# Both feed-forwards of a hybrid encoder layer by one level of Strassen's method

## The reference

```python
def swiglu(h, w_gate, w_up, w_down):
    return (jax.nn.silu(h @ w_gate) * (h @ w_up)) @ w_down

x = x + 0.5 * swiglu(rmsnorm(x, norm_ffn1), w1_gate, w1_up, w1_down)   # D_FF = 2816
x = x + token_mix(rmsnorm(x, norm_mix))      # SSD, GLA and forgetting attention, w_in and w_out
x = x + 0.5 * swiglu(rmsnorm(x, norm_ffn2), w2_gate, w2_up, w2_down)
```

## Time and profile before

| | |
|---|---|
| median of three runs | 2297.13 us |
| profiled execution: span | 2299.3 us |
| TensorE busy, matmuls | 2238.2 us (97%), 13579 |
| VectorE, ScalarE, GpSimd busy | 938.9, 537.3, 215.4 us |
| DMA: moved, mean rate | 112.34 MB, 49 GB/s |
| first feed-forward's last matmul ends | 823.9 us |
| second feed-forward's last matmul ends | 2295.6 us |

### The profile page before, as it was taken

The page is one execution under the profiler, slowest core; times in us unless marked ns, Lnnn a source line. Parts: engine busy times, 40 slices in busy tenths (PEclk is TensorE's granted clock), DMA queues, the critical chain, the costliest instruction groups (busy, mean ns, idle before and its releaser), DMA issues.

```text
span 2299.3 us, 32648 instructions
## 1 busy us (share of the span) xinstructions
PE 2238.2 (97%) x13579; PEld 2149.2 (93%) x13579; DVE 938.9 (41%) x1630; ACT 537.3 (23%) x887; POOL 215.4 (9%) x255
## 2 busy tenths in 40 slices
PE   7999999999999989999999999989999999999999
PEld 6999999999999979768889978989999999999999
DVE  5234324342243472455544294252333323333235
ACT  5211111111111252543232243231111111111110
POOL 2000000000000060231121073220000000000000
PEclk9999999999999999999999999999999999999999
DMA  4111111111111122101011103111111111111111
GB/s 152 55 38 39 36 56 55 39 37 37 56 47 46 38 79 92 58 1 37 20 39 38 42 2 124 37 37 37 55 37 56 37 37 56 37 56 37 37 56 79
DMA packets 19151, 112.34 MB, mean 49 GB/s; under 512 B 2184, under 2 KB 5736, under 8 KB 7616
## 3 DMA queue, kind: packets, MB, share of 16 engines
q1 hardware_dynamic: 16800, 97.04, 12.2%
q0 software_dynamic: 2208, 13.14, 1.5%
HBM read 98.40 MB, written 11.77 MB: 48 GB/s over the span
## 4 chain that ended last, share of the span: by engine, by line
PE 91%; DVE 5%; ACT 2%; issue 2%; POOL 1%; DMA 0%; DVEq 0%; POOLq 0%; ACTq 0%
PE ps L126 83%; DVE sb_nrm L228 2%; PE ps L650 2%; PE ps L689 2%; PE ps L662 1%; DVE sb_nl L214 1%; DVE sb_seg L1334 1%; PE ps L632 0%; ACT sb_whi L108 0%; PE ps L1150 0%; POOL sb_rms L154 0%; PE ps L949 0%; PE ps L927 0%; DVE sb_seg L1374 0%; PE ps L618 0%
## 5 line engine op out<-in xcount | busy, mean ns | idle before, releaser
L126 PE MATMUL ps<-sb_nh,sb_whi 128*128 128x362 f32 (+1 forms) x2808 | 929.7, 331 | 26.6 <-ACT sb_sg L346 8.4
L126 PE MATMUL ps<-sb_nl,sb_whi 128*128 128x362 f32 (+1 forms) x2808 | 924.8, 329 | 0.0
L126 PE MATMUL ps<-sb_nh,sb_wlo 128*128 128x362 f32 (+1 forms) x2808 | 924.8, 329 | 0.0
L126 PEld LDWEIGHTS ps<-sb_nh,sb_whi 128*128 128x128 f32 x2808 | 531.6, 189 | 36.4 <-issue 11.4
L126 PEld LDWEIGHTS ps<-sb_nl,sb_whi 128*128 128x128 f32 x2808 | 531.9, 189 | 0.5 <-issue 0.3
L126 PEld LDWEIGHTS ps<-sb_nh,sb_wlo 128*128 128x128 f32 x2808 | 531.3, 189 | 0.0
L380 DVE TENSOR_TENSOR sb_h<-sb_sg,ps 128x364 f32<-128x364 f32 x132 | 70.1, 533 | 759.4 <-PE ps L126 657.5
L393 DVE SCALAR_TENSOR_TENSOR sb_x<-ps,sb_x 128x364 f32<-128x364 f32 x528 | 276.4, 533 | 177.2 <-PE ps L126 177.2
L126 PE MATMUL ps<-sb_hh,sb_whi 128*128 128x362 f32 (+1 forms) x1056 | 345.4, 327 | 0.0
L126 PE MATMUL ps<-sb_hl,sb_whi 128*128 128x362 f32 (+1 forms) x1056 | 344.7, 326 | 0.0
L126 PE MATMUL ps<-sb_hh,sb_wlo 128*128 128x362 f32 (+1 forms) x1056 | 344.2, 326 | 0.0
(11 more groups left out here) (225 smaller groups left out, 1372.0 us busy)
## 6 DMA issues: line engine op xcount, KB each, us to landing
sb_wraw<-weights SPq DMA_DIRECT2D x83, 1024.0 KB, 4.9
x_kept<-sb_x POOLq DMA_DIRECT2D x1, 4352.0 KB, 14.3
sb_x<-x_kept POOLq DMA_DIRECT2D x4, 1088.0 KB, 10.1
out_y<-sb_x SPq DMA_DIRECT2D x8, 544.0 KB, 2.7
sb_x<-x SPq DMA_DIRECT2D x2, 1448.0 KB, 12.8
sb_x<-x SPq DMA_DIRECT2D x1, 1456.0 KB, 6.7
out_k<-sb_fk POOLq DMA_DIRECT2D x1, 1088.0 KB, 7.1
out_v<-sb_fv POOLq DMA_DIRECT2D x1, 1024.0 KB, 5.4
```

What stands on the lines that cost most here:

```text
L126: mm = K.nc.tensor.matmul(out, a, b, start=first and n == 0, stop=last and n == 2)
```

## The change

Each feed-forward's two matrix products are computed as 2 x 2 blocks with seven block products instead of eight (Strassen's form with Winograd's sums for the up part, Strassen's own for the down part). Tokens are cut in two halves of 544, each computed as two matmul streams of 272 columns.

**Up part.** The features of x (k) are halved (4 tiles each), tokens are halved, and the "rows" are gate and up of one column tile. For the first column tile (c = 0) the four results are made directly (`up_first_pe`, 4 products of 48 matmuls). For each of the other 21 tiles there are seven products P1, P2, P6, P5, P7, P3, P4 of 2 streams x 4 k x 3 = 24 matmuls. The sums of activations (T1 to T4) are made once, on VectorE, at the head (`xsum_dve`); the sums of weights per tile (`up_sum`, four of 128 x 512). P6, P7 and P4 accumulate onto the bank of P1, P3 onto that of P5, after ScalarE has copied what is needed of it (`kept`); VectorE makes three sums per tile (`summed`) and the two gated rows, which GpSimd stores to device memory (`h_kept`, 0.56 MB per tile). A ring of four holds the split weights.

x itself is overwritten by its normalized values (`items_dve`), and read back from device memory later: from the input in the first feed-forward, from `x_kept` in the second, into which SyncE saves it during the `w_out` steps.

**Down part.** The inner dimension of 22 tiles is halved (11), the 8 output tiles are halved (4), tokens are halved. Seven products of four groups; a group is one output tile: 2 streams x 11 k x 3 = 66 matmuls into a pair of banks. `DOWN` lists for each product its weight terms, its activation terms and the updates of x (sign, output half, token half). Weights come by SyncE as blocks of 128 x 1408 (0.72 MB), one or two per group; activations come by GpSimd from `h_kept` in six chunks per product (five of 128 x 1088, one of 128 x 544), one or two terms each, into two staging buffers. VectorE makes the sums and low halves, ScalarE the high halves, one product ahead. There are no hardware loops. Both feed-forwards share one set of semaphores, with the counts of the first as a base for the second. The layout of SBUF is written out by hand.

Elsewhere: x is loaded in quarters of 272 tokens, both first quarters ahead of the first weights; the constants for the mixers are loaded after the second normalization; the squares for the middle normalization follow the updates in the order in which output tiles become final. The projections, the mixers and `w_out` keep their work.

The diff, cut to its core:

```diff
+DOWN = (
+    (((1, 1, 0), (1, 1, 1)), ((1, 0, 0),), ((1, 1, 0), (-1, 1, 1))),
+    (((1, 1, 0), (-1, 0, 0)), ((1, 0, 0), (1, 0, 1)), ((1, 1, 1),)),
+    (((1, 0, 0),), ((1, 0, 1), (-1, 1, 1)), ((1, 0, 1), (1, 1, 1))),
+    (((1, 0, 0), (1, 1, 1)), ((1, 0, 0), (1, 1, 1)), ((1, 0, 0), (1, 1, 1))),
+    (((1, 1, 1),), ((1, 1, 0), (-1, 0, 0)), ((1, 0, 0), (1, 1, 0))),
+    (((1, 0, 0), (1, 0, 1)), ((1, 1, 1),), ((-1, 0, 0), (1, 0, 1))),
+    (((1, 0, 1), (-1, 1, 1)), ((1, 1, 0), (1, 1, 1)), ((1, 0, 0),)),
+)
...
+CHUNKS = tuple((k, min(k + 2, KF)) for k in range(0, KF, 2))
+NCH = len(CHUNKS)
+CHUNKS_AT = ((0, 1), (2, 3), (4,), (5,))
...
+def items_dve(K, e, N, gain, rstds):
+    for i in range(2 * KT):
+        k, cols, q, kk = item(K, i)
+        if i == KT:
+            item_lo(K, e, N, i - 1)
+        if i % KT == 0:
+            e.wait_ge(N.f.rstd, N.was.rstd + rstds[i // KT])
+        K.nc.vector.scalar_tensor_tensor(out=K.x[:, k, cols], in0=K.x[:, k, cols],
+                                         scalar=K.vec[:, gain + k:gain + k + 1], in1=K.rms[:, cols],
+                                         op0=ALU.mult, op1=ALU.mult).then_inc(N.f.nrm, 1)
+        if i % KT:
+            item_lo(K, e, N, i - 1)
+    item_lo(K, e, N, 2 * KT - 1)
...
+def up_pe(K, e, N):
+    for n in range(FIRST, PRODUCTS):
+        c, q = product_at(n)
+        y = 2 * (c % 2)
+        e.wait_ge(N.f.alo, N.was.alo + n + 1)
+        if c == 1 and q in (P6, P5, P7, P4):
+            e.wait_ge(N.f.xlo, N.was.xlo + 2 * KT + {P6: 2, P5: 4, P7: 6, P4: 8}[q])
+        if q == P1:
+            if c == 1:
+                e.wait_ge(N.f.silu, N.was.silu + 2)
+            elif c == 2:
+                e.wait_ge(N.f.h, N.was.h + 2)
+            else:
+                e.wait_ge(N.f.h, N.was.h + 2 * (c - 2) + 1)
+        elif q == P2 and c > 1:
+            e.wait_ge(N.f.summed, N.was.summed + 3 * (c - 1) - 2)
+        elif q == P6:
+            e.wait_ge(N.f.kept, N.was.kept + 3 * c - 2)
+        elif q == P5:
+            if c == 1:
+                e.wait_ge(N.f.h, N.was.h + 1)
+            else:
+                e.wait_ge(N.f.summed, N.was.summed + 3 * (c - 1))
+        elif q == P7:
+            e.wait_ge(N.f.kept, N.was.kept + 3 * c - 1)
+        elif q == P3:
+            e.wait_ge(N.f.kept, N.was.kept + 3 * c)
+        elif q == P4:
+            e.wait_ge(N.f.summed, N.was.summed + 3 * c - 1)
+        bank = {P1: y, P6: y, P7: y, P4: y, P2: 4, P5: 6, P3: 6}[q]
+        fresh = q in (P1, P2, P5)
+        for h in range(2):
+            for k in range(4):
+                cols, w = slice(Q * h, Q * h + Q), slice(P * k, P * k + P)
+                mm = three(K, K.ps[:, bank + h, :Q], K.ahi[:, n % RING, w], K.alo[:, n % RING, w],
+                           K.xh[:, q, k, cols], K.xl[:, q, k, cols], fresh and k == 0, k == 3, loose=True)
+        mm.then_inc(N.f.prod, 1)
...
+def up_start_act(K, e, N, after=None):
+    for i in range(KT):
+        item_hi(K, e, N, i)
+        if after:
+            after(i)
+    for i in range(KT, KT + 4):
+        item_hi(K, e, N, i)
+    e.wait_ge(N.f.prod, N.was.prod + 1)
+    silu(K, e, N, pair(K.c11), bank2(K, 4))
+    for i in range(KT + 4, 2 * KT):
+        item_hi(K, e, N, i)
+    up_hi(K, e, N, 4)
+    up_hi(K, e, N, 5)
+    e.wait_ge(N.f.prod, N.was.prod + 3)
+    silu(K, e, N, pair(K.g2_first), bank2(K, 2))
+    xsum_hi(K, e, N, X_T2, 0)
+    xsum_hi(K, e, N, X_T2, 1)
+    up_hi(K, e, N, 6)
+    xsum_hi(K, e, N, X_T1, 0)
+    xsum_hi(K, e, N, X_T1, 1)
+    up_hi(K, e, N, 7)
+    xsum_hi(K, e, N, X_T3, 0)
+    xsum_hi(K, e, N, X_T3, 1)
+    xsum_hi(K, e, N, X_T4, 0)
+    xsum_hi(K, e, N, X_T4, 1)
...
+def up_act(K, e, N):
...
+def up_start_dve(K, e, N):
+    gated(K, e, N, 0, 0)
+    xsum_dve(K, e, N, X_T1, 0)
+    xsum_dve(K, e, N, X_T1, 1)
+    up_sum(K, e, N, 1, 0)
+    up_lo(K, e, N, 4)
+    up_lo(K, e, N, 5)
+    xsum_dve(K, e, N, X_T2, 0)
+    xsum_dve(K, e, N, X_T2, 1)
+    up_sum(K, e, N, 1, 1)
+    xsum_lo(K, e, N, X_T2, 0)
+    xsum_lo(K, e, N, X_T2, 1)
+    gated(K, e, N, 0, 1)
+    up_sum(K, e, N, 1, 2)
+    up_lo(K, e, N, 6)
+    xsum_lo(K, e, N, X_T1, 0)
+    xsum_lo(K, e, N, X_T1, 1)
+    up_sum(K, e, N, 1, 3)
+    up_lo(K, e, N, 7)
+    xsum_dve(K, e, N, X_T3, 0)
+    xsum_dve(K, e, N, X_T3, 1)
+    xsum_dve(K, e, N, X_T4, 0)
+    xsum_dve(K, e, N, X_T4, 1)
+    xsum_lo(K, e, N, X_T3, 0)
+    xsum_lo(K, e, N, X_T3, 1)
+    xsum_lo(K, e, N, X_T4, 0)
+    xsum_lo(K, e, N, X_T4, 1)
...
+def up_pool(K, e, N, hs, x_src):
+    def store(c):
+        e.wait_ge(N.f.h, N.was.h + 2 * c + 2)
+        if c > 1:
+            e.wait_ge(N.f.hst[c % 2], N.was.hst[c % 2] + 16 * (c // 2))
+        e.dma_start(hs[c], K.h_first[:] if c == 0 else K.hbuf[:, c % 2]).then_inc(N.f.hst[c % 2], 16)
+    def first_chunk(ch):
+        k0, k1 = CHUNKS[ch]
+        if ch > 1:
+            e.wait_ge(N.f.hclo, N.was.hclo + ch - 1)
+        e.dma_start(K.est[ch % 2][:, :(k1 - k0) * HALF].rearrange("p (k t) -> p k t", k=k1 - k0),
+                    hs[k0:k1, :, 0:HALF].rearrange("k p t -> p k t")).then_inc(N.f.hld[ch % 2], 16)
+    for c in range(FT - 1):
+        store(c)
+    e.wait_ge(N.f.xlo, N.was.xlo + 2 * KT + 8)
+    e.wait_ge(N.f.hst[0], N.was.hst[0] + 16 * 6)
+    e.wait_ge(N.f.hst[1], N.was.hst[1] + 16 * 5)
+    for ch in range(NCH):
+        first_chunk(ch)
+    store(FT - 1)
+    e.wait_ge(N.f.hst[0], N.was.hst[0] + 16 * 11)
+    e.wait_ge(N.f.hst[1], N.was.hst[1] + 16 * 11)
+    e.wait_ge(N.f.hclo, N.was.hclo + NCH)
+    e.dma_start(K.x[:, 4:8], x_src[:, 4:8]).then_inc(N.f.xl[1], 16)
...
+def down_sp(K, e, N, wd):
+    e.wait_ge(N.f.xlo, N.was.xlo + 2 * KT + 8)
+    for g in range(GROUPS):
+        p, d = divmod(g, 4)
+        if g == 1:
+            e.wait_ge(N.f.alo, N.was.alo + PRODUCTS)
+        elif g == 2:
+            e.wait_ge(N.f.prod, N.was.prod + PRODUCTS)
+        elif g > 2:
+            e.wait_ge(N.f.blo, N.was.blo + g - 1)
+        done = N.f.bwe if g == 0 else N.f.bw[(g - 1) % 2]
+        for t, (_, mu, kappa) in enumerate(DOWN[p][0]):
+            e.dma_start(down_raw(K, g, t), wd[kappa, 4 * mu + d]).then_inc(done, 16)
...
+def chunk_pool(K, e, N, hs, n):
+    p, ch = divmod(n, NCH)
+    k0, k1 = CHUNKS[ch]
+    if n < NCH + 2:
+        e.wait_ge(N.f.prod, N.was.prod + PRODUCTS)
+    else:
+        e.wait_ge(N.f.hclo, N.was.hclo + n - 1)
+    for t, (_, kappa, tau) in enumerate(DOWN[p][1]):
+        e.dma_start(chunk_raw(K, n, t).rearrange("p (k t) -> p k t", k=k1 - k0),
+                    hs[KF * kappa + k0:KF * kappa + k1, :, HALF * tau:HALF * tau + HALF]
+                    .rearrange("k p t -> p k t")).then_inc(N.f.hld[n % 2], 16)
...
+def down_pe(K, e, N):
+    for g in range(GROUPS):
+        p, d = divmod(g, 4)
+        hi, lo = down_slot(K, g)
+        bank = 2 * (g % 4)
+        e.wait_ge(N.f.blo, N.was.blo + g + 1)
+        if g == 0:
+            e.wait_ge(N.f.h, N.was.h + 2 * (FT - 2) + 1)
+        elif g == 1:
+            e.wait_ge(N.f.h, N.was.h + 2 * (FT - 1) + 1)
+        elif g == 2:
+            e.wait_ge(N.f.summed, N.was.summed + 3 * (FT - 1) - 2)
+        elif g == 3:
+            e.wait_ge(N.f.summed, N.was.summed + 3 * (FT - 1))
...
+def down_act(K, e, N, follow=None):
+    for g in range(GROUPS):
+        p, d = divmod(g, 4)
+        if g + 1 < GROUPS:
+            down_hi(K, e, N, g + 1)
+        if p + 1 < NP:
+            for ch in CHUNKS_AT[d]:
+                chunk_hi(K, e, N, NCH * (p + 1) + ch)
+        if follow:
+            follow(g)
...
+def down_update(K, e, N, g):
+    p, d = divmod(g, 4)
+    e.wait_ge(N.f.grp, N.was.grp + g + 1)
+    for sign, mu, tau in DOWN[p][2]:
+        if p < 3:
+            e.wait_ge(N.f.xl[mu], N.was.xl[mu] + 16)
+        x = pair(K.x[:, 4 * mu + d, HALF * tau:HALF * tau + HALF])
+        K.nc.vector.scalar_tensor_tensor(out=x, in0=bank2(K, 2 * (g % 4)), scalar=0.5 * sign, in1=x,
+                                         op0=ALU.mult, op1=ALU.add).then_inc(N.f.x_upd, 1)
...
+def down_dve(K, e, N, last=None):
+    for g in range(GROUPS):
+        p, d = divmod(g, 4)
+        if g:
+            down_update(K, e, N, g - 1)
+        if g + 1 < GROUPS:
+            down_sum(K, e, N, g + 1)
+        chunks = [NCH * (p + 1) + ch for ch in CHUNKS_AT[d]] if p + 1 < NP else []
+        for n in chunks:
+            chunk_sum(K, e, N, n)
+        if g + 1 < GROUPS:
+            down_lo(K, e, N, g + 1)
+        for n in chunks:
+            chunk_lo(K, e, N, n)
+        if last and g == GROUPS - 1:
+            last()
+    down_update(K, e, N, GROUPS - 1)
...
+def down_pool(K, e, N, hs, x_src):
+    for n in range(NCH, NP * NCH):
+        if n == NCH + 2:
+            e.wait_ge(N.f.grp, N.was.grp + 1)
+            e.dma_start(K.x[:, 0:4], x_src[:, 0:4]).then_inc(N.f.xl[0], 16)
+        chunk_pool(K, e, N, hs, n)
```

1043 lines of the change are left out of this document (651 added, 392 removed).

## The result

| | median | runs | ratio to before, 95% interval |
|---|---|---|---|
| before | 2297.63 us | 12 | |
| changed kernel | 2303.41 us | 12 | 1.0021 [1.0012, 1.0029] |

The change costs 5.8 us where 27 were forecast as a gain; the range, 2232 to 2316, holds the time, the direction is wrong. The profiled execution has a span of 2297.5 us against 2299.3 before, 1.8 us less, although the median is 5.8 us more. The list of runs explains this. In every run of it the time is 1.8 us more than the span. The profiled execution of the changed kernel was its fastest, 2299.27 us, 4.1 under its median (the runs reach from 2299.27 to 2304.95); that of the kernel before, with 1.8 us on its span, took 2301.1 us, 3.5 over its median. What makes one execution of the same kernel some us longer than another no view shows.

A forecast was written before the change was run, and what follows sets the result against it. TensorE's matmuls (busy 97%) were taken as the bound. Changes of -11.6 (first feed-forward), +0.8, +2.8, -18.9 (second) and -0.4 summed to -27.3 us; 2297.1 - 27 = 2270 us, range 2232 to 2316.

The forecast's parts named there:

- matmul of 272 columns: TensorE: 126.5 ns each, from 119.6 ns at 256 columns plus 16 x 0.430 ns; 704.4 us per feed-forward.
- first item on VectorE: Start of each feed-forward: first normalized item of x begins at 19.8 us in the first, its start delayed 2.8 in the second.
- stall before the first P6: Head of up part: TensorE waits 8.1 us because ScalarE's copy of P1 stands behind the casts of T3 and T4.
- the loops: Written-out loops instead of hardware loops: neither cost nor give more than the 3 to 4 us TensorE idled before.
- Rival (c): Matmul price has a floor from the overlapped weight load: 130 ns, 19.5 us more per feed-forward, 2309 us; chance 0.06.
- the seams: Between and around feed-forwards: middle squares' tail +0.8 us, second one's wait for x's save +2.8, final tail -0.4.
- the stalls of the down part, its 62 us: Down part: chained chunk loads and VectorE sums make seven products take 295.8 us, 62 over 233.8 of pure matmuls.
- the forecast's own slope: Down part: each us of extra chunk-load latency costs 14 us per feed-forward.
- Rival (a): Down part: chunk loads slower, from VectorE starving GpSimd's descriptors or a lower rate; 2326 us at 2 us latency; chance 0.22.
- Its mild form: Down part: DMA rate of 358 GB/s, 14 us longer per feed-forward, 2299 us; 0.04 of the chances, counted within no change.
- its form with one us of extra latency: Down part: chunk loads land 1 us later, 14 us more per feed-forward; the latency from which it decides.
- DMA share: Heavy down products: above 0.8 if right; below 0.7 with products above 50 us would show slower chunk loads.

The follow-up runs named there:

- e3: Changed kernel with each down-part weight load, from the fourth group of each round on, cut to 128 of 1408 columns, products not the reference's: 2248.42 us.
- e4: Changed kernel with down-part queues exchanged, chunk loads issued by SyncE and most weight loads by GpSimd, waits unchanged: 2309.75 us.
- e14: Changed kernel plus third staging buffer, weights first, later chunks in product one, earlier P1 copy, x updated between weight sum and low half from product two: 2191.70 us.
- e13: Changed kernel plus third staging buffer, weights first, later chunks in product one, chunk and weight loads cut short (products not the reference's): 2194.24 us.

## Why the prediction was wrong

Step by step, forecast against the trace of the changed kernel:

| term | forecast | first | second |
|---|---|---|---|
| matmul of 272 columns | 126.5 ns | 126.0 | 126.1 |
| first item on VectorE (second: 1491.2 + 2.8 - 11.6 + 0.8) | 19.8; 1483.2 | 20.3 | 1495.2 |
| from first item to the end of the up part | 496.7; 489.7 | 498.4 | 487.1 |
| stall before the first P6 | 8.1 us | 8.5 | 8.5 |
| down part | 295.8 us | 305.9 | 311.9 |
| last matmul | 812.3; 2268.7 | 824.6 | 2294.3 |

The price of a matmul, from the chain (start, us, what), 3456 in 435.38 us, and the seam ahead of the second feed-forward:

```profile
80.50 435.38 PE ps L165 x3456
```

```profile
1490.28 4.92 DMA x_kept<-sb_x
1495.23 1.48 DVE sb_x L384 x2
```

- **Right: TensorE's price, the loops and VectorE's unit costs.** At 126.0 ns the 5568 matmuls come to 702 us per feed-forward, 704.4 in the forecast. Rival (c), a floor of the weight load, falls. VectorE's 1088 columns take 1.21 us from start to start (605.23 to 606.44 above), 1.20 in the forecast. ScalarE's line was read too low: it gives 1.80 us for the 2048 columns that took 1.9, and the casts of 1408 and 1088 columns took 1.37 and 1.10 us, not 1.27 and 1.00.
- **Right: the up part.** No wait in its body (433.00 busy of 433.00), the head with the named stall and releaser. It is 1.7 us over and 2.6 us under in the two.
- **Right: the seams.** The save of x landed at 1495.20 where about 1494 was said, and from the first feed-forward's last matmul to the second's first item the trace is within 0.3 us of the sum.
- **The step that failed: the stalls of the down part, its 62 us.** The order of the stalls and their releasers were as said (before the second group 10.9 us against 10.0, behind the chunk sum that waits for a DMA), but 305.9 - 233.8 = 72 and 311.9 - 233.8 = 78 us came. That is 10.1 and 16.1 us in a sum whose net was 27; with the 0.5 and 1.7 of the first head, less 2.6 of the second, and 0.3 of the middle, it makes the 25.5 us by which the last matmul is late, and the span 2297.5 instead of 2272. TensorE was idle some 53 and 57 us in the two down parts, against 46 in the forecast; the slower clock behind the stalls took some 18 and 20 (what is left of the busy time above 233.8), against 16.
- **What was mis-sized in it: the landings of the chunk loads.** Not the rate: 396 GB/s over both queues, 400 was taken. Nor GpSimd's descriptors (e3, e4). In the second iteration of a heavy product the forecast put half of the weights' bytes on the chunks' account and said that the last load lands 9.2 us in and the iteration takes 14.3; in the second product it was 9.1 and 14.25 (596.13 to 605.20 and to 610.38). But in the first iteration it said 6.0 us for the second chunk's load and 11.1 to 12.4 for the iteration. Two weight loads had been issued just before it, at 580.53 and 580.90, and the load landed 8.9 us in; the iteration took 14.1 (582.05 to 596.13). VectorE's timeline of it, and the load in the chain:

```profile
582.05 1.36 DVE L856 SCALAR_TENSOR_TENSOR sb_x<-ps,sb_x 128x544 f32<-128x544 f32 x2 [0.92 <-PE ps L165]
584.86 1.28 DVE L780 TENSOR_TENSOR sb_h_raw<-sb_h_raw 128x1088 f32<-128x1088 f32 x1
590.98 1.29 DVE L780 TENSOR_TENSOR sb_h_raw<-sb_h_raw 128x1088 f32<-128x1088 f32 x1 [4.83 <-DMA sb_h_raw<-h_kept]
...
582.16 8.80 DMA sb_h_raw<-h_kept
```

- **Where the 10 and 16 us lie.** By product, the first feed-forward is 2.4, 1.0, 3.9, 1.0, -0.2, 2.2 and -0.2 us over the forecast, the second 5.8, 1.0, 5.4, 2.5, -0.2, 1.7 and -0.2. So the first iteration above costs the second product only some 1.0 us; more lies in the first and the third. In the first product the second chunk's sum was to start 23 us after the up part's end. It started 25 us after it in the first feed-forward (543.92 against 518.9) and 27 in the second (2009.06 against 1982.5): the last gated row was stored at 528.4, 9.5 us after the up part's end, where about 5 was said. The third product, 37.1 in the forecast without a layout shown, took 41.0 and 42.5; its last chunk load in the second iteration landed 8.4 us in (636.35 to 644.77). By the forecast's own slope, 14 us per feed-forward and us of lateness, 10 and 16 us are worth 0.7 and 1.1 us of landing (an estimate).
- **Rival (a), slower,** had the right sign and size and the wrong mechanism: it gave a lower rate or starved descriptors. Its mild form, 2299 us with 0.04 of the chances, and its form with one us of extra latency, 2298, are nearest to the 2303.4 measured, which lies just inside what the prediction called slower (above 2301.7, 0.24). A sum that stands on a slope of 14 us per us of an unseen latency should have had a wider range of its own than 2240 to 2298.
- **DMA share.** Above 0.8 in the heavy products was said, 0.66 came. Below 0.7 was half of the prediction's sign for (a); the other half, heavy products above 50 us, did not come. It was the sign that pairs of resources wait for each other.

```profile
593.00:638.00 45.00, 39.58 (x288) 39.15 (x289) 29.96 (x27) 13.44 (x12) 10.79 (x16) 0.92 0.66 236
```

- **What is left of the 33.4 us between 2270 and 2303.4.** The 25.5 us above are the trace's. The forecast took its 27 us off the median of three runs, 2297.1, and took the span of its trace for a time near them. But around a span lie 1.8 us, so the execution of that trace took 2301.1: its last matmul belongs to a time of 2273.8, which is 3.8 us more. The last 4.1 us are those by which the profiled execution of the changed kernel lies under its median. All three go the same way, and none of them cancels another. The time is inside the range because its upper end was set for half of rival (a), whose mechanism did not come.
- **A rule.** The Trainium skill (DMA: Bandwidth & Descriptors, Where 436 GB/s comes from) has about 358 GB/s for a core from HBM; the 396 GB/s over 8.9 us above disagree, as did.

Two things are open. One is why executions of the same kernel differ by up to 5.7 us, as the changed kernel's do. The other is whether the down part should be by Strassen at all: at 165.7 ns the form before needs 1584 x 0.1657 = 262.5 us, the changed kernel's takes 305.9, and e14's 256.8, so that 5.7 us are left of the 28.7 us that seven products save on paper. The up part by Strassen with the down part of before was not tried.

## What to carry to other kernels

Fewer matmuls are worth what the other engines leave of them: where the sums and splits move to VectorE with loads ahead of them, write out one period of every queue, and look for an operation that TensorE waits for behind one that waits for a DMA. A lock-step of two resources, each about 65% full and neither at its limit, is mended by order and one more buffer (here 112 us, from 2303 to 2192, some 6 of them the head's copy, with the same operations and bytes), not by faster parts. And when the gain is the difference of a known saving and a stall whose size hangs on a latency under load, give the latency's error first: its slope may be larger than the gain. Count for a load every byte that was issued before it on any queue, and apply that in every iteration alike.

## What the hardware showed

- Loads with slack that were issued earlier take the DMA engines from urgent ones on another queue: 1.44 MB against 0.51 MB in the same 6 us, though the chunk loads were issued only 1.5 us later. With the queues exchanged (e4) the earlier loads went first too.
- GpSimd's loads show no slowing by a busy VectorE: in e13, beside a VectorE busy 29.47 of 36 us, loads of 136 KB land in 2.6 us, loads of 64 KB from SyncE in 1.9 us; the 256 KB of the earlier trace rows took 2.9. The stretch, and the landings from 580 to 700 us:

```profile
590.00:626.00 36.00, 34.48 (x275) 34.26 (x274) 29.47 (x28) 13.28 (x12) 10.86 (x16) 1.00 0.25 66
...
sb_h_raw<-h_kept POOLq DMA_DIRECT2D x33, 136.0 KB, 2.6
sb_down_raw<-wb SPq DMA_DIRECT2D x20, 64.0 KB, 1.9
```

- A VectorE sum beside GpSimd's additions takes longer: 4.57 us for 1408 columns beside three of them, 1.62 without (e13, above).
- A stall of 3 to 4 us costs more than itself. After the one that ended near 593.9 TensorE's granted clock is 0.50 (1.2 GHz) for about 3 us, then back at 2.4 GHz (changed kernel). The forecast let only stalls above 3.3 us pay for the clock; in this trace the 3 us after a stall of 3.0 us (679.2) have a mean of 0.50 too, and those after one of 4.3 us (647.7) one of 0.63:

```profile
594.00:595.00 1.00, 1.00 (x5) 1.00 (x6) 1.00 (x2) 0.00 (x0) 0.00 (x0) 0.50 0.36 62
596.00:597.00 1.00, 1.00 (x7) 1.00 (x6) 1.00 (x3) 0.00 (x0) 1.00 (x3) 0.50 1.00 406
597.00:598.00 1.00, 1.00 (x8) 1.00 (x8) 1.00 (x1) 0.00 (x0) 1.00 (x2) 0.85 1.02 389
598.00:599.00 1.00, 1.00 (x10) 1.00 (x9) 0.38 (x1) 0.59 (x1) 0.20 (x1) 1.00 1.00 408
```
